# First attention layer: both context blocks of a chunk scored together, the next chunk's near keys ahead of its context keys

## The reference

```
s_loc = einsum(q, k) * scale ; s_loc = where(mask, s_loc, -inf)
s_ctx = einsum(q, kc) * scale
p = softmax(concat[s_loc, s_ctx, sink])[..., :-1]
ox = p_loc @ v + p_ctx @ vc
# context queries: pc = softmax(concat[qc kc, sink])[..., :-1] ; oc = pc @ vc
```

## Time and profile before

| | |
|---|---|
| time, median of 3 runs | 2398.92 us (2393.33 to 2403.42) |
| the profiled execution | 2395.62 us, span 2394.3 us |
| mean granted TensorE clock | 0.989 |
| busy over the span: PE, DVE, ACT, POOL | 95%, 74%, 46%, 25% |
| the attention loop in the span | about 1712 to 1897 us |

### The profile page before, as it was taken

One profiled execution on the slowest core, in us unless ns is written; L12 is line 12 of the kernel. 1 busy time (PEld: TensorE's weight loads), 2 busy tenths in 40 slices (PEclk: granted clock), 3 DMA queues, 4 the chain that ended last, 5 costly groups with the idle time before them and its releaser, 6 DMA issues.

```text
span 2394.3 us, 34419 instructions
## 1 busy us (share of the span) xinstructions
PE 2278.7 (95%) x12827; PEld 2013.0 (84%) x12827; DVE 1779.6 (74%) x3434; ACT 1096.0 (46%) x1956; POOL 589.0 (25%) x419
## 2 busy tenths in 40 slices
PE   7989999999999998999999999999888899999997
PEld 5768999999999997999999997788655577777776
DVE  7889878878899976888887886733577645377764
ACT  4232343333488862333333335522366623566662
POOL 4110357787722232222222220200000020000001
PEclk9999999999999999999999999999999999999999
DMA  6546558888889899999999992121100012100002
GB/s 259 185 157 225 191 184 279 291 292 292 290 302 333 315 351 346 366 349 353 352 357 345 349 338 96 58 64 62 36 1 1 18 60 80 46 23 23 23 36 71
DMA packets 162374, 466.79 MB, mean 195 GB/s; under 512 B 15520, under 2 KB 72992, under 8 KB 159776
## 3 DMA queue, kind: packets, MB, share of 16 engines
q1 hardware_dynamic: 100512, 305.19, 35.7%
q0 software_dynamic: 36864, 134.23, 16.2%
q10 hardware_dynamic: 24832, 25.17, 3.3%
HBM read 412.10 MB, written 52.43 MB: 194 GB/s over the span
## 4 chain that ended last, share of the span: by engine, by line
PE 84%; DVE 6%; ACT 4%; issue 3%; DMA 2%; POOL 0%; SPq 0%; ACTq 0%; DVEq 0%; POOLq 0%
PE psum L629 7%; PE psum L630 7%; PE psum L631 7%; PE psum L491 7%; PE psum L492 7%; PE psum L493 7%; PE psum L482 6%; PE psum L484 6%; PE psum L483 6%; PE psum L602 4%; PE psum L509 3%; PE psum L978 2%; PE psum L795 2%; ACT arena L1308 1%; DVE weights_low L1536 1%
## 5 line engine op out<-in xcount | busy, mean ns | idle before, releaser
L1027 ACT ACTIVATE weights_high<-arena 128x1024 fp32r<-128x1024 f32 x355 | 374.8, 1056 | 461.6 <-PE psum L631 320.5
L1536 DVE TENSOR_TENSOR weights_low<-arena,weights_high 128x1024 fp32r<-128x1024 f32 x266 | 331.5, 1246 | 207.6 <-ACT weights_high L1027 206.6
L629 PE MATMUL psum<-hidden_high,weights_high 128*128 128x384 f32 x1024 | 343.8, 336 | 10.2 <-issue 7.8
L491 PE MATMUL psum<-x_high,weights_high 128*128 128x384 f32 x1024 | 346.5, 338 | 7.1 <-DVE weights_low L1536 7.1
L493 PE MATMUL psum<-x_high,weights_low 128*128 128x384 f32 x1024 | 342.9, 335 | 0.0
L492 PE MATMUL psum<-x_low,weights_high 128*128 128x384 f32 x1024 | 342.9, 335 | 0.0
L630 PE MATMUL psum<-hidden_low,weights_high 128*128 128x384 f32 x1024 | 342.9, 335 | 0.0
L631 PE MATMUL psum<-hidden_high,weights_low 128*128 128x384 f32 x1024 | 342.8, 335 | 0.0
L482 PE MATMUL psum<-x_high,weights_high 128*128 128x512 f32 x696 | 275.9, 396 | 14.4 <-DVE weights_low L1536 9.6
L484 PE MATMUL psum<-x_high,weights_low 128*128 128x512 f32 x696 | 271.1, 390 | 0.0
L483 PE MATMUL psum<-x_low,weights_high 128*128 128x512 f32 x696 | 271.1, 389 | 0.0
(11 more groups left out here) (263 smaller groups left out, 4301.9 us busy)
## 6 DMA issues: line engine op xcount, KB each, us to landing
arena<-in_stream SPq DMA_DIRECT2D x227, 512.0 KB, 4.5
arena<-in_v_rows SPq DMA_DIRECT2D x128, 512.0 KB, 6.7
arena<-in_ada_w SPq DMA_DIRECT2D x48, 512.0 KB, 3.5
hidden<-arena SPq DMA_DIRECT2D x128, 192.0 KB, 3.5
router<-arena SPq DMA_DIRECT2D x12, 2048.0 KB, 9.5
arena<-hidden SPq DMA_DIRECT2D x128, 192.0 KB, 7.4
arena<-router ACTq DMA_DIRECT2D x16, 1536.0 KB, 20.8
arena<-in_pair_w SPq DMA_DIRECT2D x8, 640.0 KB, 3.9
```

The source lines that it names most:

```text
L491: PE.matmul(bank[b][:, 0:N], wh[w][:, k, :], xh[:, k, PICKED:T], start=k == 0, stop=False)
L629: PE.matmul(out, wh[w][:, n, :], hh[:, r, :], start=e == 0, stop=False)
L1027: ACT.activation(wh[BUFFER[u]], slots[u % RING], AF.Copy).then_inc(*tick("weights_high", u))
L1536: DVE.tensor_tensor(wl[BUFFER[u]], slots[u % RING], wh[BUFFER[u]].bitcast(F32), ALU.subtract).then_inc(*tick("weights", u))
```

## The change

In the step of tile 3, all three engines now handle tiles 4 and 5 ahead (`A_NEXT` gives 2 and 4 for `t == 3`), and in the step of tile 4 nothing more. To let both be scored without waiting for each other, tile 4's scores go to columns 0 to 255 of the first bank with the sink in column 256, and tile 5's stay in columns 512 to 767 of the second (`a_columns`). Tile 4 therefore needs a sink copy of its own. Tile 5's scores have no wait left for exponentials. Tile 0 of the next chunk scores near keys and mask first, once tile 4's exponentials are done, and its context keys last, once tile 5's are. On DVE the gate product of part 1 moves behind the maxima of tiles 4 and 5.

```diff
+    def a_columns(t):
+        return (0, C) if t == NT else (a_tiles(t)[0], TC)
+
+    A_NEXT = {3: (2, 4), 4: ()}
...
-            if j:
-                PE.wait_ge(*at("exped", ("a", j - 2)))
-                PE.wait_ge(*at("exped", ("a", j - 1)))
+            def on_keys_of_context():
+                if j and t != NT + 1:
+                    PE.wait_ge(*at("exped", ("a", j - 2)))
+                    PE.wait_ge(*at("exped", ("a", j - 1)))
+                first = 0 if t == NT else T
+                for sc, rows in both:
+                    last = PE.matmul(sc[:, first:first + C], qr[i][rows, t * P:(t + 1) * P], kt[rows, p, T:TC], start=True,
+                                     stop=True)
+                return last
+
             if t == 0:
                 PE.wait_ge(*at("roped", ("q", i)))
+                if j:
+                    PE.wait_ge(*at("exped", ("a", j - 4)))
+                    PE.wait_ge(*at("exped", ("a", j - 3)))
+            else:
+                last = on_keys_of_context()
...
-            for sc, rows in both:
-                last = PE.matmul(sc[:, T:TC], qr[i][rows, t * P:(t + 1) * P], kt[rows, p, T:TC], start=True, stop=True)
...
+            if t == 0:
+                last = on_keys_of_context()
             last.then_inc(*tick("scored", ("a", j)))
...
-            if j + 2 < A_JOBS:
-                a_scores(j + 2)
+            for ahead in A_NEXT.get(t, (2,)):
+                if j + ahead < A_JOBS:
+                    a_scores(j + ahead)
...
         def a_exponents(j):
-            exponents("a", j, prob, a_tiles(a_job(j)[2])[0], SINK + 1, j // 2 * 2 - 4)
+            lo, hi = a_columns(a_job(j)[2])
+            exponents("a", j, prob, lo, hi + 1, j // 2 * 2 - 4)
...
-            if j + 2 < A_JOBS:
-                a_exponents(j + 2)
-                a_exponents(j + 3)
+            for ahead in A_NEXT.get(a_job(j)[2], (2,)):
+                if j + ahead < A_JOBS:
+                    a_exponents(j + ahead)
+                    a_exponents(j + ahead + 1)
             a_turn(j)
             a_turn(j + 1)
...
-                step(("sunk", j), DVE.tensor_copy(sc[:, SINK:SINK + 1], sinks[:, sink:sink + 1]))
+                step(("sunk", j), DVE.tensor_copy(sc[:, hi - 1:hi], sinks[:, sink:sink + 1]))
...
-            if i and t in (2, 3):
-                a_gates(i - 1, t - 2)
-            if j + 2 < A_JOBS:
-                a_maxima(j + 2)
-                a_maxima(j + 3)
+            if i and t == 2:
+                a_gates(i - 1, 0)
+            for ahead in A_NEXT.get(t, (2,)):
+                if j + ahead < A_JOBS:
+                    a_maxima(j + ahead)
+                    a_maxima(j + ahead + 1)
+            if i and t == 3:
+                a_gates(i - 1, 1)
```

More of the change, by code:

```diff
@@ L265, in write @@
     A_PT = [bank[4], bank[5]]
-    SINK = T + C
     cq, ckv = area(40, 4, T), area(84, 2, TC)
@@ L1915, in a_maxima @@
             i, half, t = a_job(j)
-            maxima("a", j, a_tiles(t)[0], SINK + 1, (i // 2) * 4 + 2 * (i % 2) + half if t == 0 else None,
-                   j // 2 * 2)
+            lo, hi = a_columns(t)
+            maxima("a", j, lo, hi + 1, (i // 2) * 4 + 2 * (i % 2) + half if t in (0, NT) else None, j // 2 * 2)
         def a_normalise(j):
-            normalise("a", j, prob, TC - a_tiles(a_job(j)[2])[0])
+            lo, hi = a_columns(a_job(j)[2])
+            normalise("a", j, prob, hi - lo)
         def a_gates(i, part):
```

## The result

The changed kernel takes 2414.43 us (median of 6 runs, 2412.46 to 2421.14), the kernel before 2396.45 (6 runs by now, 2390.47 to 2403.42). The ratio is 1.0081, 95% interval 1.0067 to 1.0095; the medians differ by 18.0 us. The profiled execution took 2413.14, its span 2411.8. In the after kernel the lines have moved: 752 is now 756 (context scores), 756 is 773 (near keys), 770 is 787 (mask), 787 is 806 (transposes), 816 is 835 (weighing), 1308 is 1328 (exponentials), 1327 and 1330 are 1348 and 1351 (evictions), 1905, 1906 and 1927 are 1927, 1928 and 1950 (sink, maxima, gate). An edit in an experiment moves them again by a few.

The account below looks back on a forecast made before the run. No engine is full; a ring of waits through TensorE, DVE and ACT bounds the loop. Turns 4.8, last chunk 0.9 and clock 9.1 sum to 14.8 us: 2410.4 from the profiled run, forecast 2414 near the median, range 2402 to 2422.

Parts of the forecast that it names:

- Tiles 4 and 5 scored together: TensorE before tile 3's transposes: 0.70 us of moved matmuls fit into 0.89 idle; priced at nothing, 0.7 a chunk if uncovered.
- Tile 4's transposes last: ACT's order puts these transposes behind tile 5's exponentials and tile 3's evictions, so next tile 0 scores start 0.56 us later.
- Context keys last: Tile 0's scores: near keys, mask, then context take 1.62 us against 1.50, plus 0.12 each turn between chunks.
- Last chunk: Nothing is scored next there; tile 4's transposes and all that follows on TensorE come 0.91 us later.
- Order in all: Cost of the new order across the loop: seven turns between chunks at 0.68 plus the final chunk, 5.7 us.
- DVE: Two added sink copies and earlier tile 5 reductions: maxima ready before ACT needs them; priced at nothing, at most 0.8 a chunk.
- The clock: TensorE's pause before tile 4's transposes drops its clock to half for 3.4 us: seven falls at 1.3, 9.1 us.
- rival 2: After the pauses the half clock lasts twice as long, 6.8 us: 18 for seven falls, 2423 us; chance 0.08.
- Rival 1: TensorE's clock stays full through the loop, so only the order costs: 5.7 us, 2404.6; chance 0.15.
- Rival 3: Tile 4's transposes start as before, so tile 0's scores start earlier: 0.23 a turn, 1.6 us gained, 2397; chance 0.05.

Follow-up runs that it names:

- experiment 5: Kernel before, with only tile 0's context matmuls moved behind near keys and mask; one run 2397.83 us against 2396.52, chunks 22.14 against 21.92.
- experiment 2: Changed kernel plus four useless 256-column matmuls on TensorE behind tile 3's transposes (the filled kernel); 2402.23 us, ratio 1.0024 to the kernel before.
- experiment 3: Changed kernel plus two useless 256-column matmuls on TensorE behind tile 3's transposes; one run 2402.37 us against 2396.52 for the kernel before.
- experiment 1: Changed kernel, but ACT evicts tile 3 between the exponentials of tile 4 and tile 5; 2398.69 us against 2396.2 for the kernel before, ratio 1.0012.
- experiment 6: Changed kernel, with the next chunk's tile 0 scores put ahead of tile 4's transposes on TensorE; 2392.75 us, ratio 0.9981 to the kernel before.

## Why the prediction was right, and where a size was off

The forecast was slower, 2414, for the reason that the runs show.

- *Tiles 4 and 5 scored together cost nothing.* Right: idle before tile 3's transposes went from 0.89 to 0.45, and they still started when tile 2's evictions were done.
- *Tile 4's transposes last.* Right: from the end of tile 3's transposes to tile 0's first score it was 2.26 and is 2.87 (1803.66 to 1806.53): 0.61, predicted 0.56.
- *Context keys last.* Mis-sized: 0.12 predicted, 0.22 by experiment 5. In the filled kernel the mask starts 0.64 behind the first near-key matmul (1804.91, 1805.55) where I took 0.55 from the earlier trace rows: there the near keys had run beside the end of the context pair.
- *Last chunk.* 0.91 predicted, 0.96 in experiment 2.
- *Order in all.* 5.7 predicted, for seven turns and the last chunk. Too small: a turn costs 0.82 where the clock holds (22.74 against 21.92), not 0.68. The 5.9 of experiments 2 and 3 has six turns; the first one took as long (the window 1731.30 to 1754.00 above), so the order costs 6.7.
- *DVE.* Right: four exponentials follow one another on ACT, and tile 5's start at 1803.76, 0.1 after tile 3's transposes end, not after a maximum.
- *The clock.* Right in kind and count, too small in size. Seven of the eight pauses were followed by a fall; the first one kept the full clock. I priced each at 1.3: that is what the four with 3.4 us at the low level cost (chunks of 24.0 to 24.1 against 22.74). Three stretches lasted 6.8 us, as rival 2 had it, and cost 2.8 to 2.9 each (25.6 for two of the chunks). So 13.7 instead of 9.1. I had rejected the long stretch because TensorE's work there would be dense; it was (6.68 busy of 6.70), and the clock stayed low nevertheless.
- *Rival 1, the clock holds.* It would have given 2404.6; the kernels with a filled pause are that case, at 2402.2. The Trainium skill (TensorE: Matmul & The Clock Gate, section "Why this matters for your kernels") warns only of longer idle gaps than the 2.31 here; seven falls show that shorter ones suffice where little is done around them.
- *Rival 3, near keys ahead.* Not this kernel, but its condition (ACT evicts tile 3 before tile 5's exponentials) is experiment 1, and there the near keys do get ahead: 0.14 a chunk, where I had 0.23 with 0.12 for context keys last. What I had left out is that the clock can fall after that pause of 1.35, too. Experiment 6 gains more, by changing TensorE's list as well.

The difference was 18.0 us by the medians where I had 14.8; by the traces, order and clock together are 20.4. That 2414 met the median is in part luck: both terms were too small, but with three more runs the median of the kernel before fell from 2398.92 to 2396.45.

What stays open: why the first pause, of 2.31 like the others, kept the full clock, and why three of the low stretches lasted twice as long as the other four. Those three began earliest, counted from the start of tile 4's transposes (two of them before it, one 1.1 after; 1.2 to 1.7 in the four short ones), which is an order, not a cause.

## What to carry to other kernels

When work is taken ahead on an engine with a fixed order, ask first what is queued behind it there, and who waits for that: here two exponentials that nobody needed yet stood ahead of the evictions that released the next step. A wait taken away gains only as much as what stands ahead of the waiting instruction in its own engine's list allows: 0.14 a chunk in experiment 1, where tile 4's transposes still stood ahead of the freed matmuls, 1.1 in experiment 6, where TensorE's list was changed as well. And a pause opened on TensorE is priced by what the granted clock does after it, which here cost about twice as much as the order itself (13.7 against 6.7).

## What the runs showed of the hardware that I had not expected

After the same kind of pause the low level of the clock lasted 3.4 us in four chunks and 6.8 in three of one execution, with TensorE busy nearly all of the time in both. And 1.0 us of useless matmuls in a pause of 2.4 (experiment 3) was enough in the execution traced to keep the granted clock at 1.00 after all eight pauses, at the same time of the loop as with 1.9.
